# Two first FFN tiles made together by blocks of tokens, in five of six FFNs

## The reference, cut to what matters

```python
def swiglu(x, w_gu, w_down):
    gate, up = jnp.split(x @ w_gu, 2, axis=-1)
    return (jax.nn.silu(gate) * up) @ w_down

h = h + 0.5 * swiglu(rms_norm(h, ffn1_norm[l]), ffn1_w_gu[l], ffn1_w_down[l])       # a; b likewise
x = post_norm(x, 0.5 * swiglu_2(x, ffn1_w_in[i], ffn1_w_out[i]), ln_g[i, 0], ...)   # c, e; d, f likewise
```

## Time and profile before

| | |
|---|---|
| median of 3 runs | 1676.58 us (1676.04 to 1676.81) |
| profiled execution | 1676.33 us, span 1675.0 us |
| PE busy | 1641.8 us, 98% of the span |
| DVE busy | 1193.1 us, 71% |
| ACT busy | 877.7 us, 52% |
| granted TensorE clock, mean | 0.994 |
| moved by DMA | 301.54 MB, 180 GB/s |

### The profile page before, as it was taken

The page is one execution under the profiler, slowest core; times in us unless marked ns, Lnnn a source line. Parts: engine busy times, 40 slices in busy tenths (PEclk is TensorE's granted clock), DMA queues, the critical chain, the costliest instruction groups (busy, mean ns, idle before and its releaser), DMA issues.

```text
span 1675.0 us, 24124 instructions
## 1 busy us (share of the span) xinstructions
PE 1641.8 (98%) x9630; PEld 1425.8 (85%) x9630; DVE 1193.1 (71%) x1995; ACT 877.7 (52%) x1519; POOL 46.1 (3%) x83
## 2 busy tenths in 40 slices
PE   8999999999999999999999999999999999999997
PEld 7888899778888888889878888888888998888886
DVE  6766658967666776675877676786667787676777
ACT  5544456755444454455755444655444665454445
POOL 0000000000000000001200000000000000000000
PEclk9999999999999999999999999999999999999999
DMA  9555356034555555545445554555554443554541
GB/s 370 191 188 188 138 189 239 6 134 176 189 189 189 182 211 192 192 154 224 148 158 217 192 193 178 208 184 189 189 188 183 152 145 126 202 220 188 189 164 50
DMA packets 32111, 301.54 MB, mean 180 GB/s; under 512 B 3824, under 2 KB 4352, under 8 KB 6016
## 3 DMA queue, kind: packets, MB, share of 16 engines
q1 hardware_dynamic: 32000, 300.01, 48.2%
HBM read 298.93 MB, written 1.06 MB: 179 GB/s over the span
## 4 chain that ended last, share of the span: by engine, by line
PE 88%; DVE 6%; ACT 4%; issue 1%; POOL 0%; DMA 0%; SPq 0%; DVEq 0%
PE bank L464 28%; PE bank L454 27%; PE bank L453 12%; PE bank L443 9%; PE bank L456 2%; PE bank L494 1%; DVE w_lo L427 1%; PE bank L592 1%; PE bank L2072 1%; PE bank L567 1%; DVE x L835 1%; PE bank L568 1%; PE bank L2074 1%; PE bank L571 1%; PE bank L1669 1%
## 5 line engine op out<-in xcount | busy, mean ns | idle before, releaser
L427 DVE TENSOR_TENSOR w_lo<-w_raw,w_hi 128x1024 fp32r<-128x1024 f32 (+4 forms) x539 | 586.7, 1138 | 190.9 <-ACT w_hi L420 190.5
L454 PE MATMUL bank<-xT,w_hi 128*128 128x512 f32 x1920 | 673.8, 396 | 0.0
L420 ACT ACTIVATE w_hi<-w_raw 128x1024 fp32r<-128x1024 f32 (+4 forms) x539 | 498.2, 984 | 92.2 <-PE bank L464 75.9
L453 PE MATMUL bank<-xT,w_lo 128*128 128x256 f32 x1680 | 468.4, 279 | 0.0
L454 PEld LDWEIGHTS bank<-xT,w_hi 128*128 128x128 f32 x1920 | 351.6, 188 | 69.5
L453 PEld LDWEIGHTS bank<-xT,w_lo 128*128 128x128 f32 x1680 | 316.7, 189 | 10.4
L782 ACT ACTIVATE ff_silu<-ff_silu 128x256 f32<-128x256 f32 x125 | 52.3, 418 | 388.0 <-DVE ff_silu L926 388.0
L464 PE MATMUL bank<-w_hi,hT_hi 128*128 128x512 f32 x480 | 187.5, 391 | 0.0
L464 PE MATMUL bank<-w_hi,hT_lo 128*128 128x512 f32 x480 | 186.8, 389 | 0.0
L464 PE MATMUL bank<-w_lo,hT_hi 128*128 128x512 f32 x480 | 186.8, 389 | 0.0
L926 DVE TENSOR_REDUCE ff_silu<-bank 128x256 f32<-128x512 f32 x125 | 86.3, 691 | 100.9 <-PE bank L454 99.6
(11 more groups left out here) (405 smaller groups left out, 2175.1 us busy)
## 6 DMA issues: line engine op xcount, KB each, us to landing
w_raw<-in_ffn_a SPq DMA_DIRECT2D x22, 1536.0 KB, 6.7
w_raw<-in_ffn_b SPq DMA_DIRECT2D x22, 1536.0 KB, 6.5
w_raw<-in_ffn_c SPq DMA_DIRECT2D x22, 1536.0 KB, 6.4
w_raw<-in_ffn_d SPq DMA_DIRECT2D x22, 1536.0 KB, 6.4
w_raw<-in_ffn_e SPq DMA_DIRECT2D x22, 1536.0 KB, 6.4
w_raw<-in_ffn_f SPq DMA_DIRECT2D x22, 1536.0 KB, 6.4
gains<-in_gains SPq DMA_DIRECT2D x11, 1024.0 KB, 4.8
w_raw<-in_mla_up SPq DMA_DIRECT2D x8, 1280.0 KB, 5.6
```

Source lines behind the costliest of these rows:

```text
L420: nc.scalar.activation(hi, src, ACTF.Copy).then_inc(w_hi_made, 1)
L427: nc.vector.tensor_tensor(lo, src, hi.bitcast(F32), ALU.subtract).then_inc(w_lo_made, 1)
L453: nc.tensor.matmul(o[:, 0:SEQ], lo[:, c], xT[:, k, 0, :], start=False, stop=False)
L454: ins = nc.tensor.matmul(o, hi[:, c], xT[:, k, :, :], start=(k == 0), stop=(k == KD - 1))
```

## The change

In FFNs b to f, tiles 0 and 1 are made together, by blocks, and with the tokens on the output's partitions: the turned tokens of a block are stationary and 2 x 256 columns of both tiles' gate and up weights move (`first_pair`). Each block takes 24 matmuls of 512 columns: for each half of the width, 8 that need the high parts of the tokens alone, then 4 that need the low parts. SiLU and the product with up then work on a block of 128 tokens by 256 features (`silu_of_block`, `up_of_block`), without the two reductions. The resulting h has to be turned: four transposes between gate and up of tile 2 (`turn_pair`), and then ACT and DVE split it. Down of tiles 0 and 1 follow one another behind tile 2.

Both tiles' gate and up weights are now split ahead, in all five: the high parts into the space that had tile 0's high and low parts (in c into a new one, `third_ahead`), and the low parts over the raw chunks themselves (`w_raw_lo` is the same memory as `w_raw`). So the raw slots of the two chunks are free only when the pair is made, and SP waits for it. The turn of block 0 moves into the product before in d and f too, and the six idle matmuls of e are gone. At the end of b, c's splits stand in the same order as at the end of the other FFNs.

```diff
@@ weight_stream
+        for i in (at, at + 1):
+            order.remove((i, 2))
+            order.insert(order.index((at + 2, 1)) + 1 + i - at, (i, 2))
@@ split_hi
+                before = c.before
+                if b <= GU and in_pair(chunks[before]):
+                    before = chunks[before].before
+                act.wait_ge(*freed(before, b))
@@ pe_ffn
+            def first_pair(b):
+                hi, lo = pair_hi(f), pair_lo(f)
+                o = psum[b][:, :].rearrange("p (two u) -> p two u", two=2)
+                for half in range(2):
+                    ks = range(4 * half, 4 * half + 4)
+                    for i in range(2):
+                        wait_split(pe, at + i, 0, GU // 2 * (half + 1))
+                    unit = lambda k: slice(2 * P * k, 2 * P * (k + 1))
+                    pe.wait_ge(xT_hi_made, 4 * n + 2 * b + 1 + half)
+                    for k in ks:
+                        nc.tensor.matmul(o, xT_hi[:, k, tok_of(b)], hi[:, :, unit(k)], start=(k == 0), stop=False)
+                        nc.tensor.matmul(o, xT_hi[:, k, tok_of(b)], lo[:, :, unit(k)], start=False, stop=False)
+                    pe.wait_ge(xT_lo_made, 4 * n + 2 * b + 1 + half)
+                    for k in ks:
+                        ins = nc.tensor.matmul(o, xT_lo[:, k, tok_of(b)], hi[:, :, unit(k)], start=False, stop=(k == KD - 1))
+                return ins
-            for i in range(FF_TILES):
+            if n in BY_FIRST_BLOCK:
+                if n not in TURNED_EARLY:
+                    pe_turn(n, src, (0, 1))
+                first_pair(0).then_inc(gate_up_made, 1)
+                pe_turn(n, src, (2, 3))
+                first_pair(1).then_inc(gate_up_made, 1)
+                gate_up(2)
+                down(0, 0)
+                down(0, 1)[1].then_inc(down_made, 1)
+                down(1, 0)
+                down(1, 1)[1].then_inc(down_made, 1)
+            for i in range(3 if n in BY_FIRST_BLOCK else 0, FF_TILES):
                 gate_up(i)
@@ act_ffn (dve_ffn likewise)
+            if pair:
+                silu_of_block(0)
+                split_hi(at + 2, 0)
+                split_hi(at + 2, 1)
+                silu_of_block(1)
+                split_hi(at, 2)
+                split_hi(at + 1, 2)
+                act.wait_ge(h_turned, sum(n in BY_FIRST_BLOCK for n in FFN_INPUT[:f + 1]))
+                for i in range(2):
+                    nc.scalar.activation(hT_hi[i][:, :], psum[4 + i][:, 0:SEQ], ACTF.Copy).then_inc(h_hi_made, 1)
+                split_hi(at + 2, 2)
+            for i in range(2 if pair else 0, FF_TILES - 1):
+                split_hi(at + i + 1, 0)
+                split_hi(at + i + 1, 1)
@@ the end of ffn_b on ACT (DVE likewise)
-            if FFN[f] == "ffn_b":
-
-                activate(FF_TILES - 1)
-                for i, piece in early:
-                    split_hi(i, piece)
-                return
             for i, piece in early:
                 split_hi(i, piece)
             activate(FF_TILES - 1)
@@ act_mla, and the like in the mixer, fox and before e; DVE likewise
             act_split(first["ffn_f"], 0, 2)
+            act_split(first["ffn_f"] + 1, 0, 2)
@@ pe_mla, and the like in fox
+                if (c, b, half) == (5, 1, 1):
+                    pe_turn(9, x, (0, 1))
@@ sp_program
+                        if in_pair(chunks[left]):
+                            sp.wait_ge(gate_up_made, FF_TILES * FFN.index(chunks[left].name) + 2)
                         wait_split(sp, left)
```

More of the change, by code:

```diff
@@ L241 @@
 BY_FIRST_BLOCK = (2, 3, 5, 7, 9)
+TURNED_EARLY = (2, 5, 7, 9)
 PLE_NORM = (6, 10)
@@ L356, in freed, with in_pair, pair_at @@
             }[c.name]
+        def in_pair(c):
+            return c.name in FFN and FFN_INPUT[FFN.index(c.name)] in BY_FIRST_BLOCK and c.at < 2
+        def pair_at(f, i):
+            return i if first[FFN[f]] % RAW_SLOTS < RAW_SLOTS - 1 else 1 - i
         def is_held(c, piece):
@@ L362, in is_ahead, with pair_hi, pair_lo @@
         def is_ahead(c, piece):
[L365 to L373, removed]
+            return in_pair(c) and c.pieces[piece][1] <= GU
+        def pair_hi(f):
+            return {"ffn_b": mix_ahead, "ffn_c": third_ahead, "ffn_d": fox_ahead}[FFN[f]] if f < 4 else held_w
+        def pair_lo(f):
+            slots = sorted(chunks[first[FFN[f]] + i].slot for i in range(2))
+            return raw_lo[:, slots[0]:slots[1] + 1:slots[1] - slots[0], 0:GU]
         def apart_views(c):
@@ L389, in split_views @@
             if is_ahead(c, piece):
-                return raw[c.slot][:, a:b], [w[:, a:b] for w in ahead_views(c)]
+                f = FFN.index(c.name)
+                return raw[c.slot][:, a:b], [w[:, pair_at(f, c.at), a:b] for w in (pair_hi(f), pair_lo(f))]
             return raw[c.slot][:, a:b], [w[c.pair][:, a:b] for w in (w_hi, w_lo)]
@@ L409, in split_hi @@
                 act.wait_ge(gram_made, 2 * STEPS)
+            elif is_ahead(c, piece) and c.name == "ffn_c":
+                act.wait_ge(acc_made, 8)
             elif is_ahead(c, piece) and c.name == "ffn_d":
@@ L535, in by_two_sums @@
         def by_two_sums(f, i):
-            return i < FF_TILES - 1 and (i > 0 or FFN_INPUT[f] in BY_FIRST_BLOCK)
+            return (2 if FFN_INPUT[f] in BY_FIRST_BLOCK else 1) <= i < FF_TILES - 1
         def summed_tiles(f, i):
@@ L597, in gate_up, with turn_pair @@
+            def turn_pair():
+                for b in range(TB):
+                    pe.wait_ge(h_made, FF_TILES * f + b + 1)
+                    for i in range(2):
+                        ins = nc.tensor.transpose(psum[4 + i][:, tok_of(b)],
+                                                  sig[b][:, pair_at(f, i) * P:(pair_at(f, i) + 1) * P], ident)
+                ins.then_inc(h_turned, 1)
             def gate_up(i):
@@ L957, in dve_ffn @@
             activate(FF_TILES - 1)
-            for i, piece in late[:{"ffn_a": 3, "ffn_c": 1, "ffn_e": 1}.get(FFN[f], len(late))]:
+            for i, piece in late[:{"ffn_a": 3, "ffn_b": 1, "ffn_c": 1, "ffn_e": 1}.get(FFN[f], len(late))]:
                 split_lo(i, piece)
```

113 lines of the change are left out of this document (56 added, 57 removed).

## The result

The changed kernel takes 1682.65 us (median of five runs, 1681.78 to 1684.17) against 1676.04 (1674.69 to 1676.81) of the kernel before in the same series: 1.0046 times as long, with a 95% interval of 1.0036 to 1.0057. It is slower by 6.6 us where no change was forecast (-0.1 us, a median of 1676.5), which is clear of the 3.35 us that the prediction takes for the least it could tell, and its time lies 0.65 above the range. The profiled execution took 1684.17 with a span of 1682.8; before, the span was 1675.0.

The account below looks back on a forecast made before the run. PE's work plus its waits bound the kernel. 7.7 us less work and 3 us less waiting at turns, against 10.6 us of new waits at tile 3, gave -0.1 us: a median of 1676.5, range 1669.5 to 1682.

Parts of the forecast that it names:

- The wait at tile 3: FFNs b to f: PE waits 2.12 us for tile 3's splits, queued behind tile 2's down split; 10.6 us in all five.
- The turns and the end of b: PE waits 1 to 2 us for the norm at block 0's turn before b, d, e, f; 1.8 at b's last down.
- No wait for tile 4's weights: Raw slots come free 3 to 4 us behind the pair's end, their new chunks wanted 14 us behind it or later.
- From the end of the pair to tile 3: Gate and up 5.59, transposes 0.45, down 2.72 and the splits' 4.84 make 13.60 us, against 16.63 from tile 1's old start.
- the plan's balance: Over five FFNs PE does 7.7 us less, waits 3 us less at turns, gets 10.6 back at tile 3: -0.1 us.
- The rival that two runs of 256 columns cost 0.245: In the pair, each 512 column matmul takes 0.245 us, not 0.228, as its moving side is split: 1680.6 us; chance 0.16.
- the clock falls: Rival: stops of about 2 us at tile 3 and in e lower PE's clock, 1.7 us each, five 8.5: 1685; chance 0.08.
- all five starts keep 1.00 with waits of 0.5 to 1.1 us and 1.2 to 2.2 idle in all: Argument against the clock rival: at the FFN starts of the kernel before, the clock stays full despite these waits.
- no row here shows a fall after a stop this short: Argument against the clock rival: no cited profile row shows the clock falling after a stop of about 2 us.
- Early splits find room: Rival: tile 1's parts are made without delaying block 0, turns in b, d, e, f 5.7 us earlier: 1670.8; chance 0.13.
- No wait at tile 3: Rival: the three splits ahead of tile 3 are hidden, 10.6 us less: 1665.9; chance 0.05.
- the order on ACT and rows 5, which leave no choice: Argument that tile 3 must wait: ACT's split order, and profile rows where a steady tile's three splits end 4.8 us after down.

## Why the prediction was wrong

**What held.** Each step on PE, DVE and ACT stands in the trace. The wait at tile 3: 2.05 for 2.12, five times, and its cause, the order of three splits behind down of tile 0, is shown by the run that swaps them. The turns and the end of b came within 0.2 us, with e's counted whole. No wait for tile 4's weights stands in the trace. From the end of the pair to tile 3 it takes 13.66 to 13.83 where 13.60 was worked out, and the plan's balance, PE's work down and a wait at tile 3 in its place, is +1.6 where -0.1 was forecast. Most of that, 0.3 an FFN, is the pair itself, two blocks at 0.17 each; PE in f:

```profile
1452.25 1.32 PE L522 MATMUL bank<-const,x 128*128 128x128 f32 x8 [1.57 <-DVE x L934]
...
1461.14 0.50 PE L618 MATMUL bank<-held_w,xT 128*128 128x512 f32 x1 [0.18 <-ACT xT L781]
1461.47 0.40 PE L619 MATMUL bank<-w_raw_lo,xT 128*128 128x512 f32 x1
...
1466.78 0.47 PE L482 MATMUL bank<-xT,w_hi 128*128 128x512 f32 x1
```

A block is 5.64 us from 1461.14 and not 5.47: its first matmul takes 0.33 to the next, and the other 23 stand 0.231 apart (5.31 over 23) for the 0.228 taken. The rival that two runs of 256 columns cost 0.245 is out.

**What failed** is one term: the sum put the clock's loss behind the new stops at nothing, since "the clock falls" got a chance of 0.08. In its place the profile shows five falls, 8.5 us, and the runs 5.3 us more lost to the clock than before; together with the +1.5 of the steps that is the 6.6 to within 0.2. The rival's mechanism and its price were right: stops of some 2 us at tile 3 and in e, 3.4 us at the lower level, 1.7 each. That it also had the number five is luck: it counted the five stops at tile 3, of which three had a fall, and the other two falls stand behind the end of b and e's turn.

Two pieces of evidence were held against the rival. That "all five starts keep 1.00 with waits of 0.5 to 1.1 us and 1.2 to 2.2 idle in all" has the clock right, but leaves out a longer stop, at block 1 in e:

```profile
1106.02 0.66 PE L494 MATMUL bank<-const,x 128*128 128x128 f32 x4 [1.56 <-DVE x L890]
```

Even that is shorter than any of the seven stops in question, and the forecast itself made them: 2.12 at tile 3 and, with the 0.45 that the turn waited already, 2.3 in e where the rival says "up to 1.9". And "no row here shows a fall after a stop this short" holds for the rows that were picked, not for the trace: the starts and the first product had been read for the clock, the mixer ahead of b had not. There the kernel before has these two rows on PE's timeline:

```profile
198.30 1.47 PE L494 MATMUL bank<-const,xn 128*128 128x128 f32 x8 [1.15 <-DVE xn L848]
...
301.30 0.73 PE L1144 MATMUL bank<-lent_x,mix_vals 128*64 128x256 f32 x2 [2.15 <-ACT lent_x L1363]
```

And its windows behind these stops:

```profile
198.00:204.00 6.00, 5.70 (x33) 5.14 (x33) 4.03 (x11) 3.36 (x7) 0.55 (x1) 0.72 0.00 0
...
298.00:304.00 6.00, 3.85 (x19) 2.75 (x18) 5.93 (x26) 4.01 (x18) 0.00 (x0) 0.81 0.00 1
304.00:310.00 6.00, 6.00 (x33) 5.31 (x32) 5.86 (x22) 4.94 (x16) 0.55 (x1) 0.62 0.01 3
```

Behind the first, 1.15 us ahead of the mixer's first product, the clock is 0.72 over 6 us; behind the second, 2.15 us, it is 0.81 and 0.62. The second looks like the very case that the rival asked for, but it is the weaker one, for the clock also fell in the mixer with PE at work: from 288.07, with no stop over 0.52 us in the 9 us ahead of it.

```profile
286.00:288.00 2.00, 2.00 (x13) 1.86 (x14) 2.00 (x2) 1.99 (x2) 0.00 (x0) 1.00 0.00 0
288.00:291.50 3.50, 3.50 (x17) 3.27 (x17) 3.19 (x9) 1.97 (x4) 2.34 (x6) 0.51 0.00 0
```

So at 301.30 the stop and the mixer's own work can't be told apart. Still, the first case alone has a fall behind a stop shorter than any of the new ones, and with it a chance well above 0.08 and a range up to the rival's 1685 would have followed.

The Trainium skill (TensorE: Matmul & The Clock Gate, Part 1: The HAM clock gate) has the low level for the default and activity for what lifts it. The trace agrees as far as it goes: PE fills each low stretch of the starts with matmuls and is back at 2.4 GHz after 3.41 us.

**Rivals.** *Early splits find room* was right as an idea for d, e and f (4.3 us, measured) but needed another edit than the change's. *No wait at tile 3* is what the swapped splits bring; "the order on ACT and rows 5, which leave no choice" held for the change as it stands and overlooked that the order itself could be written otherwise.

## What to carry to other kernels

On an engine that is 97% busy, a wait is not priced by its length alone: one stop of about 2 us cost its 2 us and, in two of three cases, 1.7 more of clock. When a change trades work for waits, look through the whole trace, not the changed stages alone, for stops as long as the new ones, and read the clock behind them. Where PE goes on slowly ahead of another wait, as at 288.07, the fall itself can be free. And before taking such a wait as given, look at what stands ahead in the queue of the engine that feeds it: here the piece that had to wait stood in front of two that did not.

## What the runs showed of the hardware that was not expected

A stop of PE in the midst of full work is enough for a fall of its clock, even where it is short. In the starts of the FFNs, over seven profiles (the second one of the changed kernel not counted, since it repeats the first), stops of 1.90 to 2.32 us were followed by a fall in 18 of 28 cases: 11 of 20 at tile 3, 4 of 4 at the end of b, 3 of 4 at e's turn. The fall began 0.04 to 2.33 us behind the end of the stop. Stops of 1.1 to 1.6 us had none there in seven cases, nor had the five of 1.03 to 1.56 in the kernel before, and stops filled with idle matmuls of 128 columns none in seven. Each of these falls lasted 3.41 us and cost 1.71. Yet length is not all: ahead of the mixer the stop of 1.15 us at 198.3 goes with a fall in six of eight profiles, that of before among them (in one of the six it begins in the stop's last 0.04 us), and in the mixer the clock fell with no stop over 0.52 us just ahead. Behind the same stop at the same place the clock falls in one kernel and not in another; what picks among them stays open, since no run here varied the moment alone.
